# Input stage of a two-block kernel: one small projection and the late sums computed the wide way round

## The chip, the cores and the metric

The kernel runs on one core of one Trainium2 chip. The metric is device time in microseconds (us) of one execution, the median of three runs. TensorE is called PE below, with PEld for its weight loads; DVE is VectorE, ACT is ScalarE, POOL is GpSimd and SP is SyncE, which issues most transfers.

## The reference, cut to what matters

512 tokens go through a first block (mixer, experts) and then a second one, which also reads a context of 256 tokens. The change lies in how the second block starts. Cut to that:

```
mod   = silu(c)     @ w_ada + b_ada          # 6 * 1024 values
mod_c = silu(c_ctx) @ w_ada + b_ada
sh1, sc1, g1, sh2, sc2, g2       = split(mod, 6)
sh1c, sc1c, g1c, sh2c, sc2c, g2c = split(mod_c, 6)
h  = rmsnorm(x, norm1_w)   * (1 + sc1)  + sh1
hc = rmsnorm(ctx, norm1_w) * (1 + sc1c) + sh1c
qkv, ga, ab, qb, fb2, ib, gb, mg         = split(h  @ w_in)   # ab: 32 columns of 11296
qkv_c, ga_c, ab_c, qb_c, fb2_c, ib_c, .. = split(hc @ w_in)
mix = token_mixers(...)                       # tokens only: the context's own output is not needed
x = x + g1 * mix
x = x + g2 * peer(rmsnorm(x, norm2_w) * (1 + sc2) + sh2)
```

The depth is 1, so g1c, sh2c, sc2c and g2c, the context's late two thirds of the modulation, are never used.

## The kernel before, in words

The program is seven phases in a row: mixer, route, expert, input, delta, scan, and a last one (merge and peer). Each ends with a barrier of all engines. The first third of the modulation (shift and scale) is made in the mixer phase; the input phase makes the late two thirds.

`input_phase` gathers the experts' rows and normalizes them, and then multiplies the tokens (512 columns) and the context (256 columns) by w_in_2, in output tiles of 128 rows. Exact products in f32 are made as three products of fp32r parts (`split_matmul`, L80 to L86: high by high, high by low, low by high). A class `Projection` runs a list of tiles over four weight slots: SP loads a tile (512 KB) when the product that used its slot is done, DVE cuts it into its high part (L77) and its low part (L203), PE multiplies its eight chunks, ACT evicts the product, SP stores it. There are three such stages that matter here:

- `parts`, 8 tiles, tokens only;
- `both`, 32 tiles, tokens and context: 24 products of 512 columns and 24 of 256 per tile. DVE cuts the tiles one by one and after tile k runs `modulate(k)` (L1631, L1633): for each of two chunks of w_ada_2 it multiplies 128x512 weights by silu(c) and adds them to a running sum `xT`, and the same with silu(c_ctx) into `late_context`. The eight blocks of each sum are left as sums per partition;
- `only`, 32 tiles, tokens only: 24 products of 512 columns per tile.

Between `both` and `only` PE does two small jobs. The first is the projection `ab` (L1674): for six groups of 128 tokens and eight chunks, the tokens (hT) are the stationary operand and the 32 columns of `wab` stream past. The second adds up the partitions of the modulation's sums (L1680): 64 times a 128x128 piece is the stationary operand and one column of ones streams, for tokens and context in turn. ACT copies the first result out (L1735), DVE adds the bias to the second (L1642) after its last cut, and SP stores both at the phase's end (L1546, L1548).

The order of the work is written out by hand; each engine runs its own list, and semaphores join them. `rounds` runs a body once and the rest as a loop on the engine, so `only` is one round of four tiles and a loop of seven on PE, DVE and SP.

## Time and profile before

| | |
|---|---|
| three runs, us | 4591.9, 4594.22, 4599.6; median 4594.22 |
| span of the profiled execution, us | 4552.9 |
| the profiled execution's own time beside its span | none is given; the median lies 41.3 us above the span |
| PE, PEld, DVE, ACT busy, share of the span | 91%, 77%, 73%, 45% |
| granted TensorE clock, mean over the span | 0.959 of full |
| DMA moved | 1077.84 MB, mean 237 GB/s |

Busy time is counted per engine, and PE is counted as busy also where its products are short and slow, so 91% alone says little: what a stretch is worth is read from the stage itself. The span holds everything from the first instruction to the last; what lies outside it (41.3 us) is start and end.

### The profile page before, as it was taken

How to read it: one execution, taken by the hardware profiler on the slowest of the kernel's cores; microseconds unless marked ns; L12 is line 12 of the kernel's file. 1: busy time of each engine (PE TensorE's matmuls, PEld its weight loads, DVE VectorE, ACT ScalarE, POOL GpSimd, SP SyncE). 2: the span in 40 equal slices, each digit the busy share in tenths (PEclk: the TensorE clock that was granted, in tenths of full speed). 3: DMA queues.
4: the chain of work that ended last, by engine and by line, in shares of the span. 5: the costliest groups of instructions: out<-in, count | busy, mean ns of one | idle time of the engine just before them, and what ended most of it. 6: DMA issues, size and time to landing. Idle time of an engine off the chain costs nothing. (4 is left out here: it accounts for less than half of the span.)

```text
span 4552.9 us, 59582 instructions
## 1 busy us (share of the span) xinstructions
PE 4150.0 (91%) x22056; PEld 3521.9 (77%) x22056; DVE 3308.8 (73%) x4638; ACT 2038.1 (45%) x2393; POOL 933.7 (21%) x821
## 2 busy tenths in 40 slices
PE   8987999999999779999688886998899999899997
PEld 3445777777777658898587885776699999888886
DVE  6336888888888755523488886884478894599998
ACT  1225776777777521101356554764334433233332
POOL 1010000000000000000000001100058787556664
PEclk9988999999999989989799998999899999999999
DMA  9348999999999755524301101825245545899997
GB/s 357 147 173 316 364 366 368 368 365 368 367 367 371 270 212 186 177 84 145 102 20 42 43 13 65 338 91 206 94 155 159 158 154 174 322 417 417 416 415 295
DMA packets 285455, 1077.84 MB, mean 237 GB/s; under 512 B 44628, under 2 KB 65700, under 8 KB 234372
## 3 DMA queue, kind: packets, MB, share of 16 engines
q1 hardware_dynamic: 216228, 864.25, 51.3%
q0 software_dynamic: 68832, 210.11, 11.8%
q8 instruction: 127, 2.08, 0.2%
q10 hardware_dynamic: 192, 0.79, 0.1%
q14 instruction: 76, 0.62, 0.0%
HBM read 919.40 MB, written 155.60 MB: 236 GB/s over the span
## 5 line engine op out<-in xcount | busy, mean ns | idle before, releaser
L1312 DVE TENSOR_TENSOR moe_low<-moe_raw,moe_high 128x2048 fp32r<-128x2048 f32 x256 | 574.6, 2286 | 56.0 <-ACT moe_high L1213 53.0
L3699 ACT ACTIVATE peer_high<-peer_raw 128x1024 fp32r<-128x1024 f32 x272 | 288.1, 1059 | 440.9 <-DMA peer_raw<-expert_v 399.9
L1213 ACT ACTIVATE moe_high<-moe_raw 128x2048 fp32r<-128x2048 f32 x256 | 477.8, 1905 | 0.6 <-DMA moe_raw<-w_gate_up 0.6
L3367 DVE TENSOR_TENSOR peer_low<-peer_raw,peer_high 128x1024 fp32r<-128x1024 f32 x272 | 331.5, 1220 | 125.6 <-ACT peer_high L3699 124.9
L3621 POOL DMA_INDIRECT gate_matrix<-peer_whole_gate,peer_cell x336 | 400.6, 1192 | 107.2 <-issue 105.3
L84 PE MATMUL peer_bank<-peer_hidden_high,peer_high 128*128 128x384 f32 x1024 | 354.3, 346 | 57.2 <-DVE peer_hidden_low L3489 57.2
L84 PE MATMUL peer_bank<-kept_t_high,peer_high 128*128 128x384 f32 (+1 forms) x1152 | 394.4, 342 | 9.3 <-DVE peer_low L3367 9.3
L86 PE MATMUL peer_bank<-kept_t_high,peer_low 128*128 128x384 f32 (+1 forms) x1152 | 393.6, 342 | 0.0
L85 PE MATMUL peer_bank<-kept_t_low,peer_high 128*128 128x384 f32 (+1 forms) x1152 | 393.6, 342 | 0.0
L85 PE MATMUL peer_bank<-peer_hidden_low,peer_high 128*128 128x384 f32 x1024 | 345.6, 337 | 0.0
L86 PE MATMUL peer_bank<-peer_hidden_high,peer_low 128*128 128x384 f32 x1024 | 345.5, 337 | 0.0
L1317 DVE TENSOR_TENSOR moe_low<-moe_raw,moe_high 128x2048 fp32r<-128x2048 f32 x128 | 293.0, 2289 | 66.2 <-ACT moe_high L1218 66.2
L84 PEld LDWEIGHTS peer_bank<-peer_hidden_high,peer_high 128*128 128x128 f32 x1024 | 193.8, 189 | 90.3 <-issue 61.0
L1561 POOL MEMSET zin_ident<- 128x128 f32 x1 | 0.2, 209 | 1216.0 <-POOLq L103 1216.0
L1218 ACT ACTIVATE moe_high<-moe_raw 128x2048 fp32r<-128x2048 f32 x128 | 244.2, 1908 | 0.8 <-DMA moe_raw<-w_down 0.7
L84 PE MATMUL zin_tokens<-zin_hT_high,zin_parts_w_high 128*128 128x512 f32 x576 | 228.4, 397 | 16.0 <-DVE zin_hT_low L1609 7.7
L77 DVE CAST zin_parts_w_high<-zin_parts_w 128x1024 fp32r<-128x1024 f32 x72 | 49.9, 693 | 248.0 <-DMA zin_parts_w<-w_in 248.0
L84 PEld LDWEIGHTS peer_bank<-kept_t_high,peer_high 128*128 128x128 f32 x1152 | 217.1, 188 | 15.2 <-issue 8.6
L86 PE MATMUL zin_tokens<-zin_hT_high,zin_parts_w_low 128*128 128x512 f32 x576 | 227.6, 395 | 0.0
L85 PE MATMUL zin_tokens<-zin_hT_low,zin_parts_w_high 128*128 128x512 f32 x576 | 226.5, 393 | 0.0
L1118 PE MATMUL moe_gate_bank<-moe_high,moe_x_high 128*128 128x512 f32 x512 | 210.3, 411 | 12.7 <-DVE moe_low L1312 12.7
L85 PEld LDWEIGHTS peer_bank<-kept_t_low,peer_high 128*128 128x128 f32 x1152 | 217.0, 188 | 5.4
(614 smaller groups left out, 10460.9 us busy)
## 6 DMA issues: line engine op xcount, KB each, us to landing
moe_raw<-w_gate_up SPq DMA_DIRECT2D x256, 1024.0 KB
moe_raw<-w_down SPq DMA_DIRECT2D x128, 1024.0 KB, 7.5
peer_raw<-expert_u SPq DMA_DIRECT2D x128, 512.0 KB
peer_raw<-expert_v SPq DMA_DIRECT2D x128, 512.0 KB
zin_parts_w<-w_in SPq DMA_DIRECT2D x80, 512.0 KB, 3.8
rows<-mix_zero POOLq DMA_DIRECT2D x12, 2048.0 KB, 19.3
gate_matrix<-gla_zeros POOLq DMA_DIRECT2D x32, 768.0 KB, 34.1
hidden<-peer_gelu SPq DMA_DIRECT2D x128, 192.0 KB, 1.9
```

What stands on the lines that cost most here:

```text
L77: return eng.tensor_copy(high, x)
L84: pe.matmul(out, wh, xh, start=start, stop=False)
L85: pe.matmul(out, wh, xl, start=False, stop=False)
L86: return pe.matmul(out, wl, xh, start=False, stop=stop)
L1118: pe.matmul(out[:], sh[:, c], w[:, part][:, q * 512:(q + 1) * 512], start=False, stop=False, skip_group_check=True)
L1213: act.activation(high[:, gu_slot[j]], raw[:, gu_slot[j]], ACT.Copy).then_inc(gu_high, 1)
L1218: act.activation(high[:, dn_slot[j]], raw[:, dn_slot[j]], ACT.Copy).then_inc(dn_high, 1)
L1312: v.tensor_tensor(low[:, slot], raw[:, slot], high[:, slot].bitcast(F32), ALU.subtract).then_inc(gu_low, 1)
L1317: v.tensor_tensor(low[:, slot], raw[:, slot], high[:, slot].bitcast(F32), ALU.subtract).then_inc(dn_low, 1)
L3367: v.tensor_tensor(low_part[:, slot], raw[:, slot], high[:, slot].bitcast(F32), ALU.subtract).then_inc(cut_low, 1)
L3621: pool.indirect_dma_start(out=cells, out_offset=at_cell, in_=source[:, t, h * TOPK + k:h * TOPK + k + 1], in_offset=None).then_inc(scatter ...
L3699: act.activation(high[:, k % 4], raw[:, k % 4], ACT.Copy).then_inc(cut_high, 1)
```

## The change

The context's late sum is dropped: one running sum, one small transfer less (c_ctx_2), and the late modulation gets a scratch tensor of its own without the context's half. The remaining sums over partitions are turned round: a 128x128 matrix of ones is stationary and 512 columns of the running sum stream, eight products in all, one between each two rounds of `only`; every row of the result is then the whole sum, and DVE keeps the diagonal of each 128x128 piece (`pick`: a product with the identity, then a reduction). The projection `ab` is turned round too: `wab`, cut into fp32r parts, is stationary with its 32 columns, and tokens and context stream past with 512 and 256 columns; ACT copies the 32 rows out and six transposes bring them back to the old layout. For the jobs between its rounds, `only` is written out in full on PE and DVE.

```diff
-                    for q in range(2):
-                        total = late_sum[q][:, b]
-                        if c:
-                            v.wait_ge(late_steps, 4 * k + 2 * n + q - 1)
-                            ins = v.scalar_tensor_tensor(total, late_w[:, k % 4, n], silu_c[:, c, q:q + 1], total, ALU.mult, ALU.add)
+                    total = late_sum[:, b]
+                    if c:
+                        v.wait_ge(late_steps, 2 * k + n)
+                        ins = v.scalar_tensor_tensor(total, late_w[:, k % 4, n], silu_c[:, c:c + 1], total, ALU.mult, ALU.add)
...
+            v.wait_ge(ab_loaded, 16)
+            v.tensor_copy(wab_high[:], wab[:]).then_inc(wab_cut, 1)
+            v.wait_ge(wab_cut, 1)
+            v.tensor_tensor(wab_low[:], wab[:], wab_high[:].bitcast(F32), ALU.subtract).then_inc(wab_cut, 1)
             for k in range(BOTH - EARLY):
                 both.cut_tile(v, k // 4, k % 4)
                 modulate(k)
-            only.cut(v)
+
+            def pick(b):
+                need(v, late_picked, 2 * b)
+                v.wait_ge(late_summed, b + 1)
+                v.tensor_tensor(blocks4(diagonal[:]), blocks4(sumx[:]), ident[:].unsqueeze(1).to_broadcast([P, ADA_COLS // P, P]),
+                                ALU.mult).then_inc(late_picked, 1)
+                v.wait_ge(late_picked, 2 * b + 1)
+                v.tensor_reduce(late[:, 4 * b:4 * b + 4], blocks4(diagonal[:]), AX.X, ALU.add).then_inc(late_picked, 1)
+
+            only.cut(v, between=lambda i: i and pick(i - 1))
+            pick(DC - 1)
...
-            for t in range(TOK // P):
-                for c in range(DC):
-                    last = pe.matmul(abank[:, t], hT[:, c, t * P:(t + 1) * P], wab[:, c], start=c == 0, stop=c == DC - 1)
-            last.then_inc(ab_done, 1)
-            pe.wait_ge(late_steps, 4 * (BOTH - EARLY))
-            for n in range(4 * DC):
-                b, j = divmod(n, ADA_COLS // P)
-                for q in range(2):
-                    last = pe.matmul(late_bank[:, n, q:q + 1], late_sum[q][:, b, j * P:(j + 1) * P], ones[:, 0:1], start=True, stop=True)
-            last.then_inc(late_summed, 1)
+            pe.wait_ge(wab_cut, 2)
+            for c in range(DC):
+                last = split_matmul(pe, ab_bank[0:AB, :], (wab_high[:, c], wab_low[:, c]), (hi[:, c], lo[:, c]),
+                                    start=c == 0, stop=c == DC - 1)
+            last.then_inc(ab_products, 1)
+            pe.wait_ge(rooted, 3)
+            for c in range(DC):
+                last = split_matmul(pe, sumx[0:AB, 0:CTX], (wab_high[:, c], wab_low[:, c]), (hic[:, c], loc[:, c]),
+                                    start=c == 0, stop=c == DC - 1)
+            last.then_inc(ab_products, 1)
             pe.wait_ge(both.taken, BOTH - EARLY)
-            only.multiply(pe)
+
+            def sum_late(b):
+                if b == 0:
+                    pe.wait_ge(late_steps, 2 * (BOTH - EARLY))
+                    pe.wait_ge(ab_rows, 2)
+                    for t in range(TOK // P):
+                        last = pe.transpose(abank[:, t], abT[0:AB, t * P:(t + 1) * P], ident[0:AB, 0:AB])
+                    last.then_inc(ab_done, 1)
+                need(pe, late_picked, 2 * b - 1)
+                pe.matmul(sumx[:], ones[:], late_sum[:, b], start=True, stop=True).then_inc(late_summed, 1)
+
+            only.multiply(pe, between=sum_late)
...
-            act.wait_ge(ab_done, 1)
-            act.activation(ab[:], abank[:], ACT.Copy).then_inc(ab_taken, 1)
+            act.wait_ge(ab_products, 1)
+            act.activation(abT[0:AB, 0:SEQ], ab_bank[0:AB, :], ACT.Copy).then_inc(ab_rows, 1)
+            act.wait_ge(ab_products, 2)
+            act.activation(abT[0:AB, SEQ:], sumx[0:AB, 0:CTX], ACT.Copy).then_inc(ab_rows, 1)
...
             for tile in range(ONLY):
+                if tile == 4:
+                    act.wait_ge(ab_done, 1)
+                    act.activation(ab[:], abank[:], ACT.Copy).then_inc(ab_taken, 1)
```

PE's list where `both` ends, before. After the loop's branch (L56) come 48 products with the tokens stationary (zin_hT, the last name in a row, is the stationary operand), then the sums in pairs, and then the first tile of `only`.

```order
L86 MATMUL zin_context<-zin_context_high,zin_parts_w_low 128x256
L56 REGISTER_ALU
L56 COMPARE_AND_BRANCH
L1674 MATMUL zin_ab_bank<-zin_wab,zin_hT 128x32 x48
L1680 MATMUL zin_sum_tokens<-zin_ones,zin_xT 128x1
L1680 MATMUL zin_sum_tokens<-zin_ones,zin_late_context 128x1
...
L84 MATMUL zin_tokens<-zin_hT_high,zin_parts_w_high 128x512
```

The same place in the changed list, and further down the end of the first round of `only` (the last name of a row is the stationary operand, the one before it streams):

```order
L86 MATMUL zin_context<-zin_context_high,zin_parts_w_low 128x256
L56 REGISTER_ALU
L56 COMPARE_AND_BRANCH
L84 MATMUL zin_ab_products<-zin_hT_high,zin_wab_high 32x512
L85 MATMUL zin_ab_products<-zin_hT_low,zin_wab_high 32x512
...
L84 MATMUL zin_sum_tokens<-zin_context_high,zin_wab_high 32x256
...
L84 MATMUL zin_tokens<-zin_hT_high,zin_parts_w_high 128x512
...
L1715 MATMUL zin_ab_bank<-zin_ident,zin_abT 128x32 x6
L1718 MATMUL zin_sum_tokens<-zin_xT,zin_ones 128x512
L84 MATMUL zin_tokens<-zin_hT_high,zin_parts_w_high 128x512
```

Between the stages now stand 24 products of 512 columns and 24 of 256; the six transposes and the first wide sum have moved behind four tiles of `only`, and the other seven sums behind the later rounds.

DVE's list at the start of `both`, before:

```order
L77 CAST zin_parts_w_high<-zin_parts_w 128x1024
L203 TENSOR_TENSOR zin_parts_w_low<-zin_parts_w,zin_parts_w_high 128x1024
L1633 TENSOR_SCALAR zin_xT<-zin_late_w,zin_silu_c 128x512
L1633 TENSOR_SCALAR zin_late_context<-zin_late_w,zin_silu_c 128x512
L1631 SCALAR_TENSOR_TENSOR zin_xT<-zin_late_w,zin_silu_c,zin_xT 128x512
L1631 SCALAR_TENSOR_TENSOR zin_late_context<-zin_late_w,zin_silu_c,zin_late_context 128x512
```

and in the changed list:

```order
L1651 CAST zin_wab_high<-zin_wab 128x256
L1653 TENSOR_TENSOR zin_wab_low<-zin_wab,zin_wab_high 128x256
L77 CAST zin_parts_w_high<-zin_parts_w 128x1024
L209 TENSOR_TENSOR zin_parts_w_low<-zin_parts_w,zin_parts_w_high 128x1024
L1647 TENSOR_SCALAR zin_xT<-zin_late_w,zin_silu_c 128x512
L1645 SCALAR_TENSOR_TENSOR zin_xT<-zin_late_w,zin_silu_c,zin_xT 128x512
```

Two of the four steps of `modulate` are gone, and the two cuts of `wab` stand ahead of the first cut of `both`.

## Rows read from the trace of the kernel before

**Rows 1.** Windows: stretch, length, busy PE, PEld, DVE, ACT, POOL; clock, DMA share, GB/s.
```profile
140.00:145.00 5.00, 5.00 (x13) 0.97 (x12) 3.24 (x6) 4.94 (x8) 0.00 (x0) 1.00 0.00 0
155.00:160.00 5.00, 5.00 (x10) 0.89 (x9) 0.00 (x0) 0.00 (x0) 0.00 (x0) 0.77 0.00 0
...
1860.00:1987.00 127.00, 127.00 (x735) 111.56 (x733) 62.83 (x82) 14.81 (x31) 0.00 (x0) 1.00 0.47 158
1987.00:2004.00 17.00, 17.00 (x96) 17.00 (x96) 1.92 (x2) 0.92 (x2) 0.00 (x0) 0.60 0.16 55
2004.00:2031.00 27.00, 27.00 (x129) 27.00 (x128) 0.00 (x0) 0.33 (x1) 0.00 (x0) 0.50 0.00 1
```

**Rows 2.** Timeline, PE between `both` and `only`: start, length, engine, line, operation.
```profile
1986.50 0.28 PE L85 MATMUL zin_context<-zin_context_low,zin_parts_w_high 128*128 128x256 f32 x1
1986.62 0.28 PE L86 MATMUL zin_context<-zin_context_high,zin_parts_w_low 128*128 128x256 f32 x1
1986.73 17.29 PE L1674 MATMUL zin_ab_bank<-zin_wab,zin_hT 128*128 128x32 f32 x96
...
2031.14 0.78 PE L84 MATMUL zin_tokens<-zin_hT_high,zin_parts_w_high 128*128 128x512 f32 x1
...
2034.69 0.39 PE L86 MATMUL zin_tokens<-zin_hT_high,zin_parts_w_low 128*128 128x512 f32 x1
2034.92 0.39 PE L84 MATMUL zin_tokens<-zin_hT_high,zin_parts_w_high 128*128 128x512 f32 x1
```

**Rows 3.** Timeline, PE in the mixer phase: a narrow stationary operand, and a wide sum.
```profile
139.82 7.03 PE L302 MATMUL mix_bank<-mix_ada_w,mix_silu_c 128*2 128x512 f32 x16
151.65 9.83 PE L302 MATMUL mix_bank<-mix_ada_w,mix_silu_c 128*2 128x512 f32 x16 [4.81 <-ACT mix_ada_rows L307]
...
172.68 1.02 PE L586 MATMUL mix_bank<-mix_z,mix_ones_d 128*128 128x512 f32 x2
173.14 0.79 PE L84 MATMUL mix_bank<-mix_y_high,mix_w_high 128*128 128x512 f32 x1
173.77 0.40 PE L85 MATMUL mix_bank<-mix_y_low,mix_w_high 128*128 128x512 f32 x1
```

**Rows 4.** Timeline, PE early in the input phase: four transposes.
```profile
1646.55 0.60 PE L1658 MATMUL zin_tokens<-zin_ident,zin_acc 128*128 128x128 f32 x4
```

**Rows 5.** Timeline, PE and DVE where `both` begins.
```profile
1725.37 0.80 PE L84 MATMUL zin_tokens<-zin_hT_high,zin_parts_w_high 128*128 128x512 f32 x1 [6.64 <-DVE zin_parts_w_low L203]
...
1721.24 0.49 DVE L1633 TENSOR_SCALAR zin_xT<-zin_late_w,zin_silu_c 128x512 f32<-128x512 f32 x1 [22.23 <-DMA zin_late_w<-w_ada]
1723.37 0.69 DVE L77 CAST zin_parts_w_high<-zin_parts_w 128x1024 fp32r<-128x1024 f32 x1
```

**Rows 6.** Timeline, SP and DVE in `only`: two loads and one cut.
```profile
2044.12 0.34 SPq L167 DMA_DIRECT2D zin_parts_w<-w_in  x1
2049.56 0.34 SPq L167 DMA_DIRECT2D zin_parts_w<-w_in  x1
...
2048.10 0.69 DVE L77 CAST zin_parts_w_high<-zin_parts_w 128x1024 fp32r<-128x1024 f32 x1 [3.52 <-DMA zin_parts_w<-w_in]
2048.83 1.22 DVE L203 TENSOR_TENSOR zin_parts_w_low<-zin_parts_w,zin_parts_w_high 128x1024 fp32r<-128x1024 f32 x1
```

**Rows 7.** Timeline, the end of the input phase: DVE, ACT and SP.
```profile
2191.41 0.22 DVE L1642 TENSOR_TENSOR zin_late_mod<-zin_sum_tokens,zin_b_ada 128x64 f32<-128x64 f32 x1
...
2207.18 0.60 ACT L1742 ACTIVATE zin_outx<-zin_tokens 128x512 f32<-128x512 f32 x1 [4.84 <-PE zin_tokens L86]
...
2208.19 0.42 SPq L1546 DMA_DIRECT2D mod<-zin_late_mod  x1
```

**Rows 8.** DVE prices elsewhere: a product read from PSUM, a reduction.
```profile
L484 DVE TENSOR_TENSOR mix_z<-mix_z,mix_bank x8: 680/682/689, 213.3 to 217.5; 128x512 f32<-128x512 f32 x8
...
L3469 DVE TENSOR_REDUCE peer_again<-peer_shared 128x16 f32<-128x512 f32 x3 | 2.1, 686 | 0.1
```

**Rows 9.** The page, DMA queues: queue, kind, packets, MB, share.
```profile
q8 instruction: 127, 2.08, 0.2%
```

More of the change, by code:

```diff
@@ L175, in loads, with multiply @@
             after(self.tiles // self.SLOTS - 1, n)
-    def multiply(self, pe, ready=None):
+    def multiply(self, pe, ready=None, between=None):
         def body(i):
@@ L195, in body @@
                 last.then_inc(self.products, 1)
-        rounds(pe, self.tiles // self.SLOTS, body)
+            if between:
+                between(i)
+        if between:
+            for i in range(self.tiles // self.SLOTS):
+                body(i)
+        else:
+            rounds(pe, self.tiles // self.SLOTS, body)
     def cut_tile(self, eng, i, n):
@@ L203, in cut_tile, with cut @@
         eng.tensor_tensor(self.low[:, n], self.slots[:, n], self.high[:, n].bitcast(F32), ALU.subtract).then_inc(self.low_made, 1)
-    def cut(self, eng, begun=0):
+    def cut(self, eng, begun=0, between=None):
         def body(i):
@@ L211, in body @@
                 self.cut_tile(eng, i, n)
-        rounds(eng, self.tiles // self.SLOTS, body)
+            if between:
+                between(i)
+        if between:
+            for i in range(self.tiles // self.SLOTS):
+                body(i)
+        else:
+            rounds(eng, self.tiles // self.SLOTS, body)
     def take(self, eng, copy):
@@ L1436, in input_phase @@
         wab = s.sb("wab", [P, DC, AB])
+        wab_high, wab_low = (s.sb(f"wab_{part}", [P, DC, AB], F32R) for part in ("high", "low"))
+        abT = s.sb("abT", [P, TOK])
+        diagonal = s.sb("diagonal", [P, ADA_COLS])
         ab = s.sb("ab", [P, TOK // P, AB])
@@ L3143, in _ @@
             load(3)
-            sp.dma_start(mod[:], d["mod"]).then_inc(small, 16)
+            sp.dma_start(mod[:], d["late_mod"]).then_inc(small, 16)
             sp.dma_start(w2[:], d["norm2_w_2"]).then_inc(small, 16)
@@ L3243, in _ @@
                 act.wait_ge(scaled, c + 1)
-                act.activation(t[:, c], t[:, c], ACT.Identity, bias=mod[:, SH2 + c, 0:1]).then_inc(t_made, 1)
+                act.activation(t[:, c], t[:, c], ACT.Identity, bias=mod[:, SH2 + c:SH2 + c + 1]).then_inc(t_made, 1)
                 act.wait_ge(t_made, c + 1)
```

52 lines of the change are left out of this document (25 added, 27 removed).

## The prediction, made before the changed kernel ran

> **What bounds the kernel now.** The page says PE busy 91% of the span, which cannot price a change in one stage. So I read the stage by windows first. In `both` (1860 to 1987 us) PE is busy 127.00 of 127.00 us at full granted clock, DVE 62.83 and ACT 14.81 [rows 1]: PE sets the time, and DVE has half the stretch to spare. Then come two stretches in which PE still counts as busy all the time, but at a granted clock of 0.60 and then 0.50 (1.2 of 2.4 GHz), while DVE and ACT do next to nothing [rows 1]. These are the two small jobs: 96 records of L1674 and then the 128 of L1680. Nothing runs beside them, so they lie on the path whole.
>
> The timeline gives their edges. The last product of `both` starts at 1986.62, the first L1674 at 1986.73, the first product of `only` at 2031.14 [rows 2]. So the two jobs hold PE for 2031.14 - 1986.73 = 44.4 us. The reader is to see two more things there. Products of 256 columns follow each other at 0.12 us (1986.50, 1986.62, 1986.73), and products of 512 columns at 0.23 us (2034.69, 2034.92), both at full clock. And `only` starts on the slow clock that the small products left behind: its first eight products take 2034.69 - 2031.14 = 3.55 us, where 8 x 0.23 = 1.84 would do, so 1.7 us more go there.
>
> The third view is DVE and PE where `both` begins. DVE has cut tile 0 and then waits 22.23 us for the first w_ada_2 weights; when they land at 1721.24 it runs the four steps of modulate(0) and can only then cut tile 1, at 1723.37. PE waits 6.64 us for this cut [rows 5]. This is the one place where DVE's work on the modulation is on PE's path.
>
> **The change part by part.**
>
> *The small jobs go from between the stages.* 44.4 us and the 1.7 us of slow restart: 46.1 us gained, if PE's clock stays up through what takes their place.
>
> *`ab` the other way round.* 24 products of 512 columns at 0.23 us are 5.5 us, and 24 of 256 columns at 0.12 us are 2.9 us: 8.4 us, all on the path. These prices are of full 128-wide stationary operands; here it is 32 wide, and the columns that stream set the price. Does a narrow stationary operand let the clock fall? The nearest rows are in the mixer phase: L302 streams 512 columns past a stationary operand of 2 columns, sixteen records in 7.03 us, and the window over them has a clock of 1.00; the next sixteen follow a pause, take 9.83 us, and the window over their larger part has 0.77 [rows 1, 3]. The first batch kept full clock, and the second got it back while only such products ran. I take full clock, and keep half clock (twice 8.4) for the range. Below nothing I see no bound: the operands are streamed at the same rate as in `both`.
>
> *The eight wide sums.* The nearest row is exact in kind: L586, f32, ones stationary, 512 columns, two records put between the same fp32r products. It starts at 172.68, and the second product behind it at 173.77, which is 0.23 after the first had its turn: 173.77 - 0.23 - 172.68 = 0.86 us [rows 3]. Seven of them stand between rounds of `only`: 6.0 us. The eighth belongs to the end (below).
>
> The Trainium skill puts it lower. Its page "Perfetto Trace Analysis", section "Engine Utilization", halves TensorE's output rate for FP32_LOW_HIGH, by which a 128x512 f32 product is estimated at 0.43 us; the seven sums would then cost 3.0 us and the time be about 3.0 us lower than my sum. The row shows two records of that length each, so the measurement decides here.
>
> *Six transposes.* Four of 128x128 take 0.60 us together, at most 0.15 each [rows 4]; six of 32 rows in, 32 columns wide: 0.9 us at most, taken whole. Together PE's path gets 8.4 + 6.0 + 0.9 = 15.3 us.
>
> *DVE in `both`.* Two of the four steps per tile go. From 1721.24 to 1723.37 four take 2.13 us [rows 5]; two take half, 1.07, and a little more since each now waits for the one right before it: 1.2. So the cut of tile 1 comes 0.9 us earlier, and PE with it. Later in the stage PE does not wait for DVE at all, and the rest of the saved DVE time buys nothing. The two cuts of `wab` (a quarter of a tile's columns, about 0.5 of 1.9 us, from the cut in rows 6) come ahead of tile 0's cut, where DVE afterwards waits 22.23 us anyway: nothing.
>
> *DVE in `only`.* Each round gets a pick: a 128x512 product read from PSUM, 0.68 us, and a reduction of 512 elements, 0.69 us [rows 8]. A cut takes 0.7 + 1.2 = 1.9 us and its tile comes every 5.44 us (2044.12 to 2049.56), so DVE has room; a load issued at 2044.12 has its cut begin at 2048.10 [rows 6]. PE needs the product of pick b-1 before sum b. Counted from the end of a round on PE, the last load of the next round is cut by 4.0 + 1.9 = 5.9 us and the pick's product done at 6.6; the sum that needs it stands four tiles later, at 0.9 + 4 x 5.44 = 22.6 us. That is 16 us of cover. The slots are no problem either: tile 0 of the next round can't be loaded before 0.9 + 5.4 us.
>
> *ACT and SP.* ACT gets two copies of 32 rows and moves the `ab` copy behind four tiles. Each is shorter than the 0.60 us of an eviction, after which ACT waits 4.84 us for PE [rows 7]: hidden. SP loses one small transfer; its list in the stages is otherwise the same. If this cover were gone, they would cost about 1.5 us.
>
> *The end of the phase.* Before, the late modulation was ready at 2191.41, and SP stored it at 2208.19, right behind the last tile [rows 7]. Now the chain is longer. ACT is released by the last product at 2207.18. The eighth sum starts 0.23 after the last product's start, which is 0.16 before its end (0.39 long [rows 2]), and runs 1.02 us [rows 3]: done at 2208.0 on the old axis. Then the pick, 0.68 + 0.69, and the bias, at most 0.22 [rows 7], with about 0.05 between each: 2209.7. The store of it goes out 1.5 us later than at 2208.19, and the store of `ab` and the barrier with it. Bounds: nothing, if the last tile's landing set the barrier, and 3 us if each of the four hand-overs costs 0.3 more.
>
> **Sum.** 46.1 - 15.3 + 0.9 - 1.5 = 30.2 us. The later phases begin behind a barrier and are the same work, apart from smaller loads of the modulation. The profiled span of 4552.9 us becomes 4522.7. No separate time of the profiled execution is given, so I take the 41.3 us between its span and the median of the runs shown, 4594.22, as the same after: 4594.2 - 30.2 = 4564.0 us.
>
> **Rivals.**
>
> *The clock falls in the narrow products.* For it: in the windows after 1987 small products brought the clock to 0.60 and 0.50 with PE busy throughout [rows 1]. Against it: there the weight loads filled the time as much as the products (17.00 of 17.00), while here the columns stream without a break, as L302's do. Price: 8.4 us more for `ab` and the 1.7 us of the slow restart stay: gain 20.1, 4574 us. Chance 11%.
>
> *PE waits at each sum for a pick* (the slower side). The place is the wait of sum b, with the next round of `only` behind it. A pick stands in DVE's list behind four cuts, whose loads wait for PE's own products. If the order were such that the sum needs the pick made in the same stretch, PE would stand 6.6 us at seven sums, and each pause might cost clock too: 46 us, gain gone, 4564 + 46 = 4610. It decides from 30.2 / 7 = 4.3 us a sum. Against it stands the cover of 16 us above, and the list, in which the sum needs only the pick of the round before. Chance 4%.
>
> *The written-out rounds are slow to fetch.* `only` was one body of four tiles run as a loop; now PE reads new code in every round. For it: nothing in the trace bounds it from above, since the loop hid it. Against it: all the instructions of the queue on the page came in 127 packets, 2.08 MB, 0.2% of the transfer engines [rows 9]. At 2 us for each of seven rounds the gain would be 16, 4578 us. Chance 5%. The Trainium skill, "Runtime: NRT & Kernel Launch", section "Instruction fetch mechanics", has code streamed ahead in blocks of 16 KiB, and a stall at a taken branch rather than in straight code; by that this rival falls away. The packets (2.08 MB / 127) are of that size.
>
> *The change does its work, but something outside the stage gives it back*: the scratch tensors stand elsewhere in memory, and the last phases live on transfers. I have no row for such a loss. Chance 6%, mostly no change.
>
> **How the numbers follow.** The forecast has 74%. Its own range is 4556 to 4571: the terms of the end (0 to 3 us for 1.5), the clock at the restarts (about 2 us either way) and the spread of three runs (4591.9 to 4599.6). The range of 8 in 10 takes in the clock rival and ends short of the third: 4554 to 4576. A change of 0.2%, 9.2 us, is about what a measurement of this kernel tells from none. Faster by more: the forecast, the clock rival and the third, with a little of the fourth, 91%. Within it 5%, slower 4%.
>
> **What would show it.** In the profile after: between the last product of `both` and the first of `only` some 8.4 us at full clock; 0.23 us from product to product at once in `only`; 0.86 us for each sum, with no idle time of PE ahead of it; PE's wait at the start of `both` near 5.7 us; the store of the late modulation some 2.5 us after ACT's release by the last product. The forecast is wrong if the span falls by less than 24 us or more than 36: by a clock below 0.9 in the narrow products, by PE waiting for DVE between rounds, or by a phase behind the input phase that changes its length by more than 3 us.

## The result, and the profile after

Over the runs of the two kernels side by side the kernel before takes 4597.03 us (median of 8, 4590.77 to 4606.54) and the changed one 4567.57 us (median of 8, 4561.52 to 4589.17). The ratio is 0.9943 with a 95% interval of 0.9930 to 0.9957: 29.5 us faster. The forecast was 4564.0 us and a gain of 30.2 us.

The span of the profiled execution tells the opposite story at first sight: 4572.3 us after, 4552.9 us before. So the first thing to do is to cut both spans into phases. A phase begins with the first start of a tile that only this phase uses. The input stretch is counted from the first product of `parts` to the first record of the phase behind it.

| us | before | after | difference |
|---|---|---|---|
| all ahead of it | 1659.7 | 1658.1 | -1.5 |
| input stretch | 552.2 | 522.6 | -29.6 |
| delta phase | 603.0 | 604.3 | +1.3 |
| scan phase | 274.7 | 273.5 | -1.2 |
| merge, start of the last phase | 165.9 | 165.7 | -0.2 |
| peer, rest of the last phase | 1297.5 | 1348.1 | +50.6 |
| span | 4552.9 | 4572.3 | +19.4 |

The input stretch gave what the medians show. The +50.6 us stand in code that the change does not touch; the first experiments deal with them.

The windows of the changed kernel from `both` to the end of `only`, in the form of [rows 1] (the column behind POOL is the granted clock):

```profile
1860.00:1985.00 125.00, 125.00 (x717) 109.39 (x716) 46.03 (x54) 13.91 (x29) 0.00 (x0) 1.00 0.48 161
1985.00:1993.20 8.20, 8.20 (x50) 5.14 (x49) 1.92 (x2) 1.57 (x3) 0.00 (x0) 1.00 0.32 112
...
2014.00:2018.00 4.00, 4.00 (x21) 2.76 (x20) 1.67 (x2) 0.82 (x2) 0.00 (x0) 1.00 0.39 100
2018.00:2174.00 156.00, 156.00 (x678) 127.01 (x677) 56.99 (x64) 16.15 (x27) 0.00 (x0) 1.00 0.42 129
```

The two windows at 0.60 and 0.50 are gone: the clock is 1.00 (2.4 GHz) from `both` through `ab` to the last tile, and PE has no idle time in any of the four. DVE has 46.03 us of work in 125 where it had 62.83 in 127 [rows 1]. PE's timeline has the edges (start, length, engine, line, operation):

```profile
1984.94 0.39 PE L84 MATMUL zin_ab_products<-zin_hT_high,zin_wab_high 128*32 128x512 f32 x1
1985.17 0.39 PE L85 MATMUL zin_ab_products<-zin_hT_low,zin_wab_high 128*32 128x512 f32 x1
...
1993.08 0.28 PE L86 MATMUL zin_sum_tokens<-zin_context_high,zin_wab_low 128*32 128x256 f32 x1
1993.19 0.40 PE L84 MATMUL zin_tokens<-zin_hT_high,zin_parts_w_high 128*128 128x512 f32 x1
1993.42 0.40 PE L85 MATMUL zin_tokens<-zin_hT_low,zin_parts_w_high 128*128 128x512 f32 x1
...
2014.75 0.39 PE L86 MATMUL zin_tokens<-zin_hT_high,zin_parts_w_low 128*128 128x512 f32 x1
2015.07 0.56 PE L1715 MATMUL zin_ab_bank<-zin_ident,zin_abT 32*128 32x32 f32 x6
2015.56 1.13 PE L1718 MATMUL zin_sum_tokens<-zin_xT,zin_ones 128*128 128x512 f32 x2
...
2038.30 1.02 PE L1718 MATMUL zin_sum_tokens<-zin_xT,zin_ones 128*128 128x512 f32 x2
2038.76 0.80 PE L84 MATMUL zin_tokens<-zin_hT_high,zin_parts_w_high 128*128 128x512 f32 x1
2039.39 0.39 PE L85 MATMUL zin_tokens<-zin_hT_low,zin_parts_w_high 128*128 128x512 f32 x1
...
2060.96 1.02 PE L1718 MATMUL zin_sum_tokens<-zin_xT,zin_ones 128*128 128x512 f32 x2
```

From the first product of `ab` to the first of `only` are now 1993.19 - 1984.94 = 8.25 us, where 44.4 stood [rows 2], and `only` goes at 0.23 us from its first product on instead of 3.55 us for the first eight. The narrow products follow each other at 0.23 and 0.11 us. A wide sum costs 2039.39 - 0.23 - 2038.30 = 0.86 us, the same to the hundredth as the row of another phase from which it was priced [rows 3]. Counted over a whole round it is a little more: from one sum to the next are 2060.96 - 2038.30 = 22.66 us, and four tiles without a sum take 4 x 5.44 = 21.76 [rows 6], so that a sum adds 0.90. The six transposes take 2015.56 - 2015.07 = 0.5 us, 0.7 counted the same way. PE has no idle time ahead of any L1718.

Where `both` begins, DVE and PE, against [rows 5]:

```profile
1723.08 0.80 PE L84 MATMUL zin_tokens<-zin_hT_high,zin_parts_w_high 128*128 128x512 f32 x1 [5.85 <-DVE zin_parts_w_low L209]
...
1719.89 0.49 DVE L1647 TENSOR_SCALAR zin_xT<-zin_late_w,zin_silu_c 128x512 f32<-128x512 f32 x1 [22.60 <-DMA zin_late_w<-w_ada]
1720.41 0.75 DVE L1645 SCALAR_TENSOR_TENSOR zin_xT<-zin_late_w,zin_silu_c,zin_xT 128x512 f32<-128x512 f32 x1
1721.08 0.68 DVE L77 CAST zin_parts_w_high<-zin_parts_w 128x1024 fp32r<-128x1024 f32 x1
```

The cut now comes 1.19 us behind the landing (1721.08 - 1719.89) where it came 2.13 behind it, and PE waits 5.85 us instead of 6.64.

The end of the phase, all engines, against [rows 7]:

```profile
2174.03 0.40 PE L86 MATMUL zin_tokens<-zin_hT_high,zin_parts_w_low 128*128 128x512 f32 x1
2174.26 1.02 PE L1718 MATMUL zin_sum_tokens<-zin_xT,zin_ones 128*128 128x512 f32 x2
...
2174.46 0.60 ACT L1784 ACTIVATE zin_outx<-zin_tokens 128x512 f32<-128x512 f32 x1 [4.85 <-PE zin_tokens L86]
...
2175.39 0.69 DVE L1661 TENSOR_TENSOR zin_diagonal<-zin_sum_tokens,zin_ident 128x512 f32<-128x512 f32 x1 [16.50 <-PE zin_sum_tokens L1718]
2176.11 0.69 DVE L1664 TENSOR_REDUCE zin_late_mod<-zin_diagonal 128x4 f32<-128x512 f32 x1
2176.91 0.19 DVE L1670 TENSOR_TENSOR zin_late_mod<-zin_late_mod,zin_b_ada 128x32 f32<-128x32 f32 x1
...
2177.12 0.33 SPq L1561 DMA_DIRECT2D late_mod<-zin_late_mod  x1
```

The store of the late modulation leaves 2177.12 - 2174.46 = 2.66 us after ACT's release, where it left 1.01 us after it. That is 1.65 us later, on the path that sets the barrier.

### The profile page after: what moved, and what is told of

It is laid out like the page before. It is cut to its first block and busy times, and to the rows that moved or that the text cites. A ratio compares the mean times of both kernels' runs of the same rounds, so it can differ in the third digit from the quotient of the medians.

```text
span 4572.3 us, 59143 instructions
## 1 busy us (share of the span) xinstructions
PE 4147.7 (91%) x21902; PEld 3495.7 (76%) x21902; DVE 3283.8 (72%) x4592; ACT 2036.7 (45%) x2395; POOL 921.2 (20%) x821
## 3 DMA queue, kind: packets, MB, share of 16 engines
q8 instruction: 130, 2.13, 0.2%
## 5 line engine op out<-in xcount | busy, mean ns | idle before, releaser
L86 PEld LDWEIGHTS peer_bank<-kept_t_high,peer_low 128*128 128x128 f32 x1152 | 221.3, 192 | 18.5 <-issue 13.1
```

What stands on the lines that cost most here:

```text
L86: return pe.matmul(out, wl, xh, start=False, stop=stop)
```

## The experiments

Each experiment is read by its input stretch, as in the table above. Repeated, the stretch came to 552.2 and 553.3 us for the kernel before (mean 552.7), and to 522.6, 523.8 and 523.9 for the changed work: about 1 us is what one profile can tell. The parts of the stretch vary more than that, from one execution to another of the same code. The 96 records of the old `ab` took 17.1, 17.7, 17.4, 15.5 and 14.7 us in the five profiles at normal clock that have them. The wait of PE for the cut of the second tile of `both` was 6.64 to 8.05 us in the four profiles with four steps of the modulation a tile, and 5.85 to 6.78 in the eight with two.

### Both kernels again on one chip, and the scratch layout

Two profiles differ by 50.6 us in a phase that both run alike. Either the last phase differs by execution or chip (theory A), or the new place of the scratch tensors slows it (theory B, the prediction's fourth rival). Both kernels ran again, unchanged, on one chip, and with them one where the scratch tensors stand where they stood before:

```diff
-    "hT": ((D, SEQ), F32), "mod": ((P, 2 * DC, 2), F32), "late_mod": ((P, 4 * DC), F32), "rows": ...
+    "hT": ((D, SEQ), F32), "mod": ((P, 6 * DC, 2), F32), "rows": ...
...
+    "late_mod": ((P, 4 * DC), F32),
 }
```

> The kernel before, unchanged, profiled a second time. In the first pair of profiles the changed kernel's input phase was 29.6 us shorter (552.2 to 522.6 us from the first product of the stage parts to the first record of the next phase), but its last phase was 50.6 us longer (1297.5 to 1348.1 us), while eight timed runs each differ by about 26 to 30 us. Theory A, the last phase varies from execution to execution whatever the kernel, and the first profile of before was a fast one: here the input stretch is 552.2 within 0.5, and the last phase lies anywhere from 1297 to 1350, most likely near 1340, so that the span is near 4595. Theory B, the change lengthens the last phase by its new scratch layout: the last phase is again 1297 within 5 us.

> The changed kernel, unchanged, profiled a second time. Theory A: input stretch 522.6 us within 0.5, last phase from 1297 to 1350 us and not the 1348 of the first profile to within 5. Theory B: last phase 1348 us within 5.

> The changed kernel with the scratch tensors in device memory where they were before: the tensor of the modulation keeps its old size, and the new one for the late part stands behind all others. Nothing else changes. Theory A: the time is that of the changed kernel, near 4566 us or 0.9943 of before, within 0.2%. Theory B (the new layout costs the last phase some 20 to 50 us): 4520 to 4548 us, a ratio of 0.984 to 0.990.

| | time, us | input | peer | PE waits for "issue" in peer |
|---|---|---|---|---|
| before, first profile | | 552.2 | 1297.5 | none |
| after, first profile | 4574.08 | 522.6 | 1348.1 | 31.2 us, 54 times |
| before, again | 4558.22 | 553.3 | 1297.9 | none |
| after, again | 4524.92 | 523.8 | 1297.2 | none |
| layout | 4527.69, median of 5 | 523.9 | 1302.8 | none |

The same program takes 1348.1 us for the peer part on one occasion and 1297.2 on the other. Theory B is out: with the new layout and with the old one the part is short here, and the old layout's ratio to the kernel before, 0.9937 [0.9924, 0.9951], agrees with the changed kernel's 0.9943 [0.9930, 0.9957]. The expectation also named a time, and 4527.69 us lies in theory B's range of times and not near the 4566 of theory A. But the kernel before is as much faster on this chip: its 9 runs beside the layout kernel have a median of 4555.58 us (4549.81 to 4560.13). Only the ratio can decide here. PE's waits in that part, first of the changed kernel's first profile:

```profile
PE peer_bank L84 <- DVE peer_hidden_low L3531: 46.1, 105, 6.1
PE peer_bank L84 <- issue: 13.1, 22, 1.6
PE peer_bank L84 <- DVE peer_low L3409: 11.6, 2, 8.6
PE peer_bank L86 <- issue: 8.8, 16, 1.6
PE peer_bank L85 <- issue: 7.3, 14, 1.0
```

and of the same kernel on the other chip (line, what it waited for, us in total, times, longest):

```profile
PE peer_bank L84 <- DVE peer_hidden_low L3531: 57.5, 91, 9.8
PE peer_bank L84 <- DVE peer_low L3409: 9.3, 2, 8.4
```

In the long one PE stops 54 times, for 0.6 us in the mean and 1.6 at most, without any semaphore that the profile shows ("issue"). Over all kernels of this study the split is clean: in the four profiles with a peer part of 1297 to 1303 us there is no such wait in it, in the nine others that ran at a normal clock (1332 to 1349 us) there are 22 to 39 us of them. The long and the short ones do not mix on one chip: the three from this chip are short, and the eight from the two chips of the experiments below are long. The times of the kernel before show the same: 4549.81 to 4560.13 us in 9 runs on this chip, 4583.41 to 4602.16 in 11 runs on one of the others. It goes with where the program ran, not with the kernel. Each chip was used on one occasion only, so that chip and occasion can't be told apart.

### Rounds written out

`only` of the kernel before, with nothing else changed than that its rounds are written out instead of run as a loop, as the change needs it.

```diff
+        only.flat = True
...
-        rounds(pe, self.tiles // self.SLOTS, body)
+        if self.flat:
+            for i in range(self.tiles // self.SLOTS):
+                body(i)
+        else:
+            rounds(pe, self.tiles // self.SLOTS, body)
```

> The kernel before with the stage only written out in full on PE and DVE, and nothing else. My theory: writing out costs and gains nothing, input stretch 552.2 us within 0.5. The rival of the slow fetch: PE stands about 1 to 2 us at each of seven rounds, 559 to 566 us. If the loop's branch cost time before, it would be below 551.

The run took 14288.01 us. It was disturbed as a whole. Its windows, in the form of [rows 1]:

```profile
0.00:600.00 600.00, 530.32 (x1872) 334.65 (x1872) 354.45 (x455) 228.31 (x226) 43.49 (x77) 0.94 0.72 279
...
1200.00:14286.00 13086.00, 12939.62 (x17803) 9457.67 (x17802) 2509.00 (x3834) 1434.36 (x1879) 804.98 (x744) 0.21 0.16 54
```

From some 1200 us on, over 400 us before the input stretch and so before any code that differs, the granted clock is 0.21, which is below both of the levels that the other runs show. The other kernels of this batch ran on the same chip with a mean clock of 0.957 to 0.965. Nothing is learned from it about the rounds, so the same kernel ran again:

> The same kernel as unroll_alone, which ran at a granted clock of 0.271 and told nothing. The kernel before with the stage only written out in full on PE and DVE. My theory: input stretch 552 to 554 us. Rival of the slow fetch: 559 to 566 us.

4585.45 us beside a median of 4589.2 of the kernel before (11 runs, 4583.41 to 4602.16); input stretch 551.3 us. That is 0.7 below the 552 to 554 expected, and it is not the rounds: `ab` took 14.7 us here instead of 17.1 and 17.7, and PE's wait in `both` 8.05 us instead of 6.64 and 6.70. The stage itself decides. From the first product of its second tile to its last product are 168.41 us written out (2032.49 to 2200.90), and 168.41 as a loop in both profiles of the kernel before (2038.34 to 2206.76 and 2040.32 to 2208.74). Written-out rounds cost nothing, and nor does the loop's branch. The third rival is refuted, as the Trainium skill's "Runtime: NRT & Kernel Launch", section "Instruction fetch mechanics", has it for straight code. The instructions of this kernel came in 131 packets (2.15 MB) and those of the changed kernel in 130 (2.13 MB), instead of 127 [rows 9].

### The parts one at a time

*The context's late sum dropped, nothing turned round.* The kernel before with one running sum:

```diff
-                    for q in range(2):
+                    for q in range(1):
...
-            pe.wait_ge(late_steps, 4 * (BOTH - EARLY))
+            pe.wait_ge(late_steps, 2 * (BOTH - EARLY))
...
-                for q in range(2):
+                for q in range(1):
                     last = pe.matmul(late_bank[:, n, q:q + 1], late_sum[q][:, b, j * P:(j + 1) * P], ones[:, 0:1], start=True, stop=True)
```

> The kernel before with only the context's late sum dropped: 64 of the 128 records of the sums go (13.6 us at 0.213 each), and half of the modulation's steps on DVE. My theory: 552.7 - 13.6 - 0.4 at the start of the stage both: 538 to 540 us. The DVE work that goes (64 steps of 0.66 us, 42 us) lies beside PE and gives no more. Rival, DVE's load slows the stage both: below 535.

The input stretch is 538.4 us: 14.3 us shorter than 552.7. PE between the stages (timeline):

```profile
1984.80 16.85 PE L1674 MATMUL zin_ab_bank<-zin_wab,zin_hT 128*128 128x32 f32 x89
2001.46 13.79 PE L1680 MATMUL zin_sum_tokens<-zin_ones,zin_xT 128*128 128x1 f32 x64
2015.11 0.77 PE L84 MATMUL zin_tokens<-zin_hT_high,zin_parts_w_high 128*128 128x512 f32 x1
```

The small sums take 2015.11 - 2001.46 = 13.65 us, half of the 27.3 they took (2003.83 to 2031.14). So half of the whole gain needs no new arithmetic: it is work whose result nobody read.

*The late sums dropped and turned round, `ab` left as it was.*

```diff
-            pe.wait_ge(wab_cut, 2)
-            for c in range(DC):
-                last = split_matmul(pe, ab_bank[0:AB, :], (wab_high[:, c], wab_low[:, c]), (hi[:, c], lo[:, c]),
-                                    start=c == 0, stop=c == DC - 1)
...
+            for t in range(TOK // P):
+                for c in range(DC):
+                    last = pe.matmul(abank[:, t], hT[:, c, t * P:(t + 1) * P], wab[:, c], start=c == 0, stop=c == DC - 1)
+            last.then_inc(ab_done, 1)
```

> The changed kernel with the projection ab as it was before (48 small f32 products between the stages). My theory: of the changed stretch (522.6, 523.8, 523.9 us in three profiles) the ab part's 17.0 - 8.3 - 0.6 = 8.1 us come back, and the slow restart of the stage only (1.7 us), since the small products lower the clock again: 532 to 534 us. If the low clock came from the sums alone, the restart would be at full clock: 531.

532.5 us, 20.2 shorter than 552.7. Against the kernel with only the drop, turning the remaining sums round is worth 5.9 us: 13.65 less between the stages, less 6.3 for seven sums and 1.6 at the end. Two more things nearly cancel: the old `ab` happened to take 15.5 us here and 17.4 there, and the tiles of `both` cost 1.6 us more here (explained below).

*`ab` turned round, the sums left as they were*, in the kernel before:

```diff
-            for t in range(TOK // P):
-                for c in range(DC):
-                    last = pe.matmul(abank[:, t], hT[:, c, t * P:(t + 1) * P], wab[:, c], start=c == 0, stop=c == DC - 1)
+            for c in range(DC):
+                last = split_matmul(pe, ab_bank[0:AB, :], (wab_high[:, c], wab_low[:, c]), (hi[:, c], lo[:, c]),
+                                    start=c == 0, stop=c == DC - 1)
...
+            for t in range(TOK // P):
+                last = pe.transpose(abank[:, t], abT[0:AB, t * P:(t + 1) * P], ident[0:AB, 0:AB])
+            last.then_inc(ab_done, 1)
```

> The kernel before with only the projection ab turned round (24 products of 512 columns and 24 of 256 past the 32 columns of wab, two copies out, six transposes behind the late sums). Input stretch before: 552.1 and 553.3 us in two profiles. My theory, terms add up: 17.0 us of old ab products become 8.3, the transposes add about 0.6 and the tail nothing, the old sums start at full clock and lose it within some 4 us (at most 1 us gained): 9 us shorter, 543 to 545. Rival, the ab part brings its gain only with the sums part, since the old sums still leave the clock low: 551 or more.

541.0 us, 11.7 shorter than 552.7 and 2 us more than expected. The windows say why (first the narrow products, then the beginning of the small sums in two pieces):

```profile
1985.00:1993.30 8.30, 8.30 (x51) 5.20 (x50) 1.92 (x2) 1.57 (x3) 0.00 (x0) 1.00 0.30 111
1993.30:2000.00 6.70, 6.70 (x55) 6.70 (x52) 0.00 (x0) 0.37 (x1) 0.00 (x0) 0.85 0.01 2
2000.00:2004.00 4.00, 4.00 (x20) 4.00 (x21) 0.00 (x0) 0.00 (x0) 0.00 (x0) 0.50 0.00 0
```

The small sums start on full clock now and keep it for a while, since no L1674 has brought it down before them. They take 23.1 us (1993.38 to 2016.45) instead of 27.3 (2003.83 to 2031.14). So the parts do not add: 11.7 + 20.2 = 31.9 us, and together they give 552.7 - 523.4 = 29.3. The kernel with `ab` alone saves 4.2 us of the small sums' time by the clock, and those sums are gone in the other kernel anyway. The 2.6 us between the two figures are less than that, and about what the varying parts of single profiles allow.

### Does a narrow stationary operand let the clock fall?

Four times the 512-column products of `ab` (each of the four passes begins its sum anew, at c == 0, so `ab` still comes out once; the expectation is wrong there):

```diff
-            for c in range(DC):
+            for c in 4 * list(range(DC)):
                 last = split_matmul(pe, ab_bank[0:AB, :], (wab_high[:, c], wab_low[:, c]), (hi[:, c], lo[:, c]),
```

> The changed kernel with the 24 narrow products of 512 columns of the projection ab done four times over, 96 in a row, so that products past a 32-wide stationary operand fill some 25 us. Their sum is then not the reference's in that part. My theory: a narrow stationary operand keeps the clock up, 72 more products at 0.227 us add 16.3 us: input stretch 539 to 541 us, granted clock 1.00 all through. Rival, the clock falls once such products have run for some us: 72 at 0.427 us and a slow restart, 24 to 33 us more, 548 to 557 us.

540.3 us, 16.9 more than 523.4, for 72 products more: 0.235 us each. The window over 24 us of them:

```profile
1982.50:2006.50 24.00, 24.00 (x115) 12.20 (x114) 1.92 (x2) 1.57 (x3) 0.00 (x0) 1.00 0.11 39
```

At 32 columns wide the clock stays at 1.00, with PEld busy half of the time. The clock rival is refuted, with room: the batch is three times as long as the one that the kernel has. The small products that brought the clock to 0.60 and 0.50 stand beside PEld at 17.00 of 17.00 and 27.00 of 27.00 [rows 1]. They keep one pace whether 32 columns stream or one: 0.11 us a record while the clock is full, 0.21 at half clock, in L1674 as in the small sums. That points at the weight loads as what sets their time. Whether it is the loads or the few columns that let the clock fall was not tested, since both differ between these products and the narrow ones.

### What if PE did wait for the picks?

The second rival, forced: each pick one round later in DVE's list. The sum then needs the pick behind the cuts that PE itself holds up.

```diff
-            only.cut(v, between=lambda i: i and pick(i - 1))
+            only.cut(v, between=lambda i: i > 1 and pick(i - 2))
+            pick(DC - 2)
             pick(DC - 1)
```

> The changed kernel with each pick one round later in DVE's list, so that PE's sum b waits for a pick that stands behind the four cuts of the next round: the wait that was priced as the slower side, 6.6 us at each sum from the second to the last but one, six or seven of them. That price: 40 to 46 us, and more if the pause costs PE its clock (8 products at half speed are 1.7 us each time, up to 12 us): input stretch 563 to 582 us. If the cover that I counted (16 us) is wrong and the changed kernel is near this wait already, the loss would be far smaller, below 20 us.

4629.25 us beside 4601.22 of the kernel before; input stretch 579.0 us, 55.6 more than the changed kernel. The waits of PE in `only`:

```profile
PE zin_sum_tokens L1719 <- DVE zin_diagonal L1661: 39.8, 6, 6.8
```

and the windows over the first such wait and what follows it:

```profile
2037.50:2044.20 6.70, 0.00 (x0) 0.00 (x0) 3.18 (x5) 0.60 (x1) 0.00 (x0) 0.70 0.37 117
2044.20:2050.60 6.40, 6.39 (x13) 4.37 (x14) 0.68 (x1) 0.00 (x0) 0.00 (x0) 0.51 0.00 0
2050.60:2062.00 11.40, 11.40 (x52) 9.41 (x51) 1.92 (x2) 1.20 (x2) 0.00 (x0) 1.00 0.39 104
```

The wait itself is 6.6 us, as the prediction had it. Behind it PE works 6.4 us at a clock of 0.51 before it has its speed back. Six waits of 6.6 are 39.8 us. From the first product of `only` to its last this kernel takes 54.7 us more than the changed one, so 14.9 us are left, 2.5 a wait, and the slow stretch behind each wait is the only other difference seen there. The remaining 0.9 us of the 55.6 lie ahead of `only`. The rival's mechanism is real and would have made the change slower; the list avoids it by one position.

### Where the two ends can be mended

*Each sum after the second tile of its round*, so that the eighth is done long before the phase ends:

```diff
                 last.then_inc(self.products, 1)
-            if between:
-                between(i)
+                if between and n == 1:
+                    between(i)
```

> The changed kernel with each wide sum (and the transposes) after the second tile of a round and not after the fourth, so that the last sum, pick and bias are done ten us before the last product. My theory: the 1.5 to 1.6 us that the longer chain costs at the end come back, and nothing else changes: input stretch 521.0 to 522.4 us. Rival, the last tile's store sets the barrier anyway: 522.6 to 524.

The end of the phase (timeline, all engines):

```profile
2173.19 0.39 PE L86 MATMUL zin_tokens<-zin_hT_high,zin_parts_w_low 128*128 128x512 f32 x1
2173.62 0.60 ACT L1784 ACTIVATE zin_outx<-zin_tokens 128x512 f32<-128x512 f32 x1 [4.84 <-PE zin_tokens L86]
...
2174.92 0.33 SPq L1561 DMA_DIRECT2D late_mod<-zin_late_mod  x1
...
2178.79 0.32 SPq L1911 DMA_DIRECT2D gdn_ab<-ab  x1
```

From the last product to the next phase are 5.6 us (2173.19 to 2178.79), against 6.66 after the change (2174.03 to 2180.69) and 5.08 before it (2206.76 to 2211.84): 1.1 us back of the 1.5 to 1.6 expected, and 0.5 us of the longer end stay, unexplained. The gain of this kind in the whole stretch, 522.5 against 522.6 to 523.9, is too small to be told from the spread, and falls between the two ranges of the expectation; the tail itself shows it.

*With it, DVE's modulation three tiles behind the cuts*, so that a cut of `both` never stands behind the wait for w_ada_2:

```diff
             for k in range(BOTH - EARLY):
                 both.cut_tile(v, k // 4, k % 4)
+                if k > 2:
+                    modulate(k - 3)
+            for k in range(BOTH - EARLY - 3, BOTH - EARLY):
                 modulate(k)
```

> The kernel of early_sum, and in the stage both DVE cuts three tiles ahead of the modulation: cuts 0 to 3, then modulate(0), cut 4, modulate(1) and so on. The wait of PE at the second tile (5.85 us after the change) and the half clock behind it (about 2.7 us) go. My theory: 8 to 9 us more than early_sum, input stretch 512 to 514 us, and a ratio near 0.9915 to before. Rival, the transfers of the modulation's weights then come later and make a wait of their own behind the first tiles: 515 or more.

514.9 us, 7.6 less than the kernel before it in this list, where 8 to 9 had been expected. The windows from the first product of `both` on, and for comparison those of the changed kernel over the same place (it starts there at 1708.61):

```profile
1705.00:1720.00 15.00, 15.00 (x86) 13.12 (x86) 3.15 (x4) 0.98 (x2) 0.00 (x0) 1.00 1.00 352
1720.00:1983.00 263.00, 263.00 (x1504) 228.05 (x1504) 103.69 (x126) 31.47 (x64) 0.00 (x0) 1.00 0.49 167
```

```profile
1708.00:1730.00 22.00, 15.54 (x79) 13.40 (x80) 9.90 (x13) 1.49 (x3) 0.00 (x0) 0.84 0.80 293
```

PE has no idle time in the stage any more and keeps full clock through it: the wait (5.95 us in the kernel before it in this list) is gone, and with it 1.7 us that were put down to the slow restart, where the expectation had 2.7. The expected rival, a new wait behind the first tiles, did not come. Timed: 4557.78 us (median of 6, 4552.8 to 4563.4) against 4589.2 of the kernel before (11 runs); ratio 0.9927 [0.9912, 0.9943]. Its 31.4 us beat the 27.9 us of the layout kernel, which does the changed work, on its chip (4555.58 - 4527.69); the two intervals of the ratio overlap, so that it is faster than the changed kernel rests on the 7.6 us of the profile more than on the times.

## Why the prediction was right, and which step was not

**The mechanism.** PE set the time between the stages, and the two small jobs lay on the path whole: of 44.4 + 1.7 us, 8.3 are left, at full clock, and the restart is gone. The experiments confirm the split: 13.65 us for half of the small sums, and `ab` turned round alone in 8.3 us.

**The sum, term by term.** Predicted and measured, each on the stage's own time, as means over the two profiles of the kernel before and the three of the changed work. The slow restart is what the first tile of `only` takes beyond the 5.47 us that it takes after the change (7.21 and 8.22 us before). The last row adds the unrounded figures.

| | predicted | measured |
|---|---|---|
| small jobs gone | +44.4 | +44.7 (44.4 and 45.0) |
| slow restart gone | +1.7 | +2.2 (1.7 and 2.8) |
| `ab` the other way round | -8.4 | -8.25 |
| seven wide sums | -6.0 | -6.3 (0.90 each) |
| six transposes | -0.9 | -0.7 |
| start of `both` earlier | +0.9 | +0.75 |
| tiles of `both` slower | none | -1.6 |
| the end of the phase | -1.5 | -1.6 |
| sum | +30.2 | +29.3 |

The input stretch as a whole gives the same 29.3 (552.7 - 523.4) and the medians 29.5 (4597.03 - 4567.57). That the sum came out within 1 us owes something to luck: the jobs, the restart and the transposes gave about 1 us more than priced, and so hid part of the 1.6 us that the prediction did not have. The forecast of 4564.0 is 3.6 us below the measured 4567.57: 2.8 of it because the kernel before came out at 4597.03 over 8 runs instead of 4594.22 over 3, 0.7 from the sum.

**The earlier cut, and a cost that the prediction did not have.** The earlier cut was to give 0.9 us. Counted from the first product of `parts`, the eviction of the second tile of `both` starts at 76.86 and 76.40 us in the two profiles before, at 75.01, 76.28 and 76.35 in the three of the changed work: 0.75 us earlier in the mean, with 1.3 us between executions of one kernel. Over all profiles in which `both` is written in this order it is 0.9: the mean is 77.1 us in the four with four steps of the modulation a tile (76.40 to 77.62) and 76.1 in the eight with two (75.01 to 76.75). So the term was right. But the evictions of the last tile start at 327.26 and 326.80 before, and at 327.00, 328.28 and 328.35 after. The gain is not only lost, it has turned into a loss of 0.85. In between nobody waits, and the clock is 1.00. What differs is the tile itself. Two of ACT's evictions, 24 tiles apart, before:

```profile
1761.57 0.60 ACT L1731 ACTIVATE zin_out<-zin_tokens 128x512 f32<-128x512 f32 x1 [7.33 <-PE zin_context L86]
...
1961.89 0.60 ACT L1731 ACTIVATE zin_out<-zin_tokens 128x512 f32<-128x512 f32 x1 [7.33 <-PE zin_context L86]
```

and in the changed kernel, 24 tiles apart as well:

```profile
1758.35 0.60 ACT L1768 ACTIVATE zin_out<-zin_tokens 128x512 f32<-128x512 f32 x1 [7.39 <-PE zin_context L86]
...
1959.95 0.60 ACT L1768 ACTIVATE zin_out<-zin_tokens 128x512 f32<-128x512 f32 x1 [7.39 <-PE zin_context L86]
```

A tile of `both` takes (1961.89 - 1761.57) / 24 = 8.347 us before and (1959.95 - 1758.35) / 24 = 8.400 after, and every single tile does so, to a hundredth. 30 tiles make 1.6 us. In `only` a tile without a sum takes 5.44 us in both kernels. The prediction had priced `both` from DVE's side alone: fewer steps can't make it slower. The experiments narrow it down: 8.347 also with the rounds written out, with the drop alone and with `ab` alone; 8.400 in every kernel that has the sums turned round (the sums alone, the old scratch layout, all later ones). What these share, apart from the sums themselves, which run only later, is among other things that three small tensors that lie ahead of the operands of `both` in the on-chip memory are 192 bytes per partition smaller (silu(c), its source and the late modulation without the context's half; the other new tensors are multiples of 1 KB). They also lack the tensor of the context's sum, which every kernel at 8.347 still has in memory. That the operands' place causes it is a guess, not shown: no kernel was run that changes this alone.

**The wide sums.** The row of two records decided, and rightly. By the rate in the Trainium skill's "Perfetto Trace Analysis", section "Engine Utilization", the estimate was 3.0 us for seven sums; 0.86 to 0.90 us each is twice that, because each product is two records of 0.43.

**The rivals.** The clock in the narrow products: refuted by four times as many at 1.00. PE waiting for a pick: did not happen, and forced it cost 55.6 us, more than the 46 said, since each wait takes 2.5 us more behind it. The written-out rounds: the same 168.41 us, no cost. The scratch layout: no difference that the ratios show.

**The step that failed** is "so I take the 41.3 us between its span and the median of the runs shown, 4594.22, as the same after", and with it the sentence of what lies outside the span as start and end. The executions show what does lie outside: 4574.08 us for a span of 4572.3, 4558.22 for 4556.5, 4601.22 for 4599.5, always 1.7 or 1.8 us. The rest of the 41.3 fits the peer part, which was short in the profiled execution (1297.5 us). A span of 4552.9 with 1.7 us more is 4554.6 us, among the 4549.81 to 4560.13 of the chip where the part is short, while the first 8 timed runs lie from 4590.77 to 4606.54. That the part was long in those is inferred, since they have no profile. The step did no harm to the forecast because the same number was added and taken away. It did harm to the test that the prediction set: "the forecast is wrong if the span falls by less than 24 us or more than 36". The span rose by 19.4 us while the kernel got 29.5 us faster. By its own rule the prediction would have been called wrong. The last of its conditions, a later phase that changes its length by more than 3 us, was the right one to look at, and the runs on one chip show that it was not the change. Of the terms of the sum, the one that failed is `both`: it was priced from DVE's side alone and put at no loss, and each of its tiles became 0.053 us slower.

**Open.** Why a tile of `both` takes 0.053 us more (above). What makes the peer part 1297 us on one chip and 1332 to 1349 on others. The stops of PE for "issue" go with it in all thirteen profiles, and add up to 22 to 39 of the 35 to 51 us; what they wait for the profile does not show, and no experiment on it was made. Whether the weight loads or the few columns of the small products bring the clock down.

## What to carry to other kernels

A batch of tiny matrix products between two dense stages costs more than its columns: it runs at the weight loads' pace, lets the clock fall, and leaves the next stage a slow start; make the small operand the stationary one, or spread wide products between the rounds of dense work. Before that, ask whether anyone reads the result: half of this gain came from a sum that was never used. And compare two profiles phase by phase, and stage by stage the tile's period, before you compare their spans: here the span and the time moved in opposite directions.

## What the hardware showed that was not expected

- The same program on two chips: 1348.1 and 1297.2 us in the same part of 1300 us. That is 1.1% of the whole time, more than the effect of this change, so kernels must be compared on one chip and in one batch.
- A plain f32 product of 128x512 with a 128-wide stationary operand costs 0.86 us among fp32r products of 0.23: nearly four times as much. Counted over a round it is 0.90.
- 96 products of 512 columns with a stationary operand 32 wide, and then 24 of 256, kept the clock at 1.00 for over 20 us. In another kernel, products of one column with a stationary operand 128 wide stood right behind 24 and 24 such products, and the clock did not hold: 0.85 and then 0.50.
- The 48 products of a tile of `both` take 8.347 us in one kernel and 8.400 in another, steadily, with the same shapes, order and clock.
- A wait of 6.6 us costs PE some 2.5 us more behind it, in products at the slow level.
- The same 96 small products took from 14.7 to 17.7 us in five executions, by where among them the clock fell.
- One execution of 14288 us with a granted clock of 0.21 over 13 ms, below both levels that all others show. The same kernel ran normally on another chip, and other kernels of its batch ran normally on the same chip.
